# Order of the work inside a step of the projection: bank copies and weight splits before the head norms

## What is computed

```
h = rms_norm(x, g_mix)
proj = h @ w_in            # q, k, v of 3 groups of 8 heads | 512 SSM channels | gate_a | gate_b
q = head_rms_norm(q) * 64**-0.5      # t * rsqrt(mean(t*t) + eps), 64 columns of a head at a time
k = head_rms_norm(k)
sigmoid(gate_a), sigmoid(gate_b)
```

## Time and profile before

| | |
|---|---|
| time, median of 3 runs | 4731.93 us (4725.41, 4731.93, 4736.51) |
| span of the profiled execution | 4720.7 us |
| the profiled execution's own time | not listed beside the runs; the median lies 11.2 us above its span |
| busy: TensorE matmul, weight load, VectorE, ScalarE, GpSimd | 4550.3, 3984.6, 3161.5, 2181.6, 923.1 us |
| granted TensorE clock, mean | 0.985 |
| the projection | 0 to about 1204 us |

### The profile page before, as it was taken

How to read it: one execution, slowest core, us unless ns; L and a number is a source line. 1 busy time by engine, 2 the same in 40 slices (tenths; PEclk the granted TensorE clock), 3 DMA queues, 4 the chain that set the end, 5 groups by cost and what they waited for, 6 DMA issues and landing times.

```text
span 4720.7 us, 76711 instructions
## 1 busy us (share of the span) xinstructions
PE 4550.3 (96%) x25756; PEld 3984.6 (84%) x25756; DVE 3161.5 (67%) x6216; ACT 2181.6 (46%) x3608; POOL 923.1 (20%) x911
## 2 busy tenths in 40 slices
PE   8999999999899989996999999999999999999998
PEld 6777787777789978785999999999988888999997
DVE  6668676674656678455555565666667777778887
ACT  4454444343256752232333343444445555556665
POOL 2332101444112001122011111111112111111111
PEclk9999999999999999998999999999999999999999
DMA  6887766555644445443455456565657657777777
GB/s 214 283 310 266 229 200 204 165 188 176 209 165 147 140 162 187 163 146 124 164 187 190 167 187 204 172 213 192 210 200 238 215 206 245 246 249 268 271 270 255
DMA packets 339406, 971.18 MB, mean 206 GB/s; under 512 B 42089, under 2 KB 75668, under 8 KB 301909
## 3 DMA queue, kind: packets, MB, share of 16 engines
q1 hardware_dynamic: 273784, 804.16, 48.3%
q0 software_dynamic: 28304, 88.03, 8.0%
q10 hardware_dynamic: 37085, 76.04, 4.5%
HBM read 772.82 MB, written 200.58 MB: 206 GB/s over the span
## 4 chain that ended last, share of the span: by engine, by line
PE 51%; DVE 1%; ACT 0%; issue 0%; DVEq 0%; POOL 0%; DMA 0%; ACTq 0%; SPq 0%; POOLq 0%
PE ex_d L2834 14%; PE ex_g L2801 11%; PE ex_g L2803 9%; PE ex_g L2797 7%; PE ex_d L2797 4%; PE ex_d L2828 3%; PE ex_d L2803 2%; PE ex_g L2778 1%; PE ex_d L2778 0%; DVE ex_x L2996 0%; PE ex_d L2809 0%; DVEq L2605 0%; ACT ex_wgh L2881 0%; ACT ex_x L2894 0%; DVE ex_y L3070 0%
## 5 line engine op out<-in xcount | busy, mean ns | idle before, releaser
L2803 PE MATMUL ex_g<-ex_x,ex_wgl 128*128 128x256 f32 (+12 forms) x3456 | 981.7, 284 | 0.0
L2801 PE MATMUL ex_g<-ex_x,ex_wgh 128*128 128x288 f32 (+5 forms) x3584 | 757.1, 303 | 2.4 <-DVE ex_x L2996 2.4
L2803 PEld LDWEIGHTS ex_g<-ex_x,ex_wgl 128*128 128x128 f32 x3456 | 653.6, 189 | 3.9
L2881 ACT ACTIVATE ex_wgh<-ex_wg 128x2048 fp32r<-128x2048 f32 x274 | 523.9, 1912 | 283.0 <-PE ex_g L2803 275.6
L2978 DVE TENSOR_TENSOR ex_wgl<-ex_wg,ex_wgh 128x2048 fp32r<-128x2048 f32 x274 | 626.7, 2287 | 41.3 <-ACT ex_wgh L2881 41.3
L2801 PEld LDWEIGHTS ex_g<-ex_x,ex_wgh 128*128 128x128 f32 x3584 | 593.8, 188 | 11.6 <-DVE ex_x L2996 2.8
L2797 PE MATMUL ex_g<-ex_x,ex_wgh 128*128 128x512 f32 (+6 forms) x1664 | 529.6, 377 | 1.0 <-DVE ex_t L3008 1.0
L699 PE MATMUL prj_p<-prj_wh,prj_ah 128*128 128x512 f32 x1136 | 453.1, 399 | 28.4 <-DVE prj_wl L902 22.8
L2746 POOL DMA_INDIRECT out<-ex_y,ex_cur x82 | 155.4, 1896 | 1509.4 <-ACT ex_y L2902 1241.7
L699 PE MATMUL prj_p<-prj_wh,prj_al 128*128 128x512 f32 x1136 | 446.1, 393 | 0.0
L699 PE MATMUL prj_p<-prj_wl,prj_ah 128*128 128x512 f32 x1136 | 445.9, 393 | 0.0
(11 more groups left out here) (453 smaller groups left out, 9483.2 us busy)
## 6 DMA issues: line engine op xcount, KB each, us to landing
ex_wg<-in_w_gu SPq DMA_DIRECT2D x276, 1024.0 KB, 5.1
ex_wd<-in_w_down SPq DMA_DIRECT2D x276, 512.0 KB, 6.2
qkv_d<-prj_o ACTq DMA_DIRECT2D x144, 256.0 KB, 2.6
sp_rows<-sums_d SPq DMA_DIRECT2D x125, 256.0 KB, 3.1
wo_spare<-qkv_d SPq DMA_DIRECT2D x40, 768.0 KB, 4.2
sp_rows<-in_w_in SPq DMA_DIRECT2D x113, 256.0 KB, 3.1
sp_early<-in_w_in SPq DMA_DIRECT2D x56, 512.0 KB, 5.5
sums_d<-sp_early SPq DMA_DIRECT2D x28, 1024.0 KB, 5.3
```

What stands on the lines that cost most here:

```text
L2801: pe.matmul(out[:, 0:size], h[:, k, j, :], x[:, k, 0:size], start=(k == 0 and x is xh), stop=False)
L2803: last = pe.matmul(out[:, 0:size], l[:, k, j, :], xh[:, k, 0:size], start=False, stop=(k == KD - 1))
L2881: act.activation(flat(wgh[f % 2][:, :, :, :]), flat(wg[f % RAW][:, :, :, :]), ACT.Copy).then_inc(wgh_ready, 1)
```

## The change

In the loop over g, ScalarE calls `leave` and `split` first, and roots, gates and squares behind them. VectorE calls `leave` and `split` first, and scales and means behind them. Nothing else is changed: the same instructions with the same semaphores, in another order.

```diff
 # ScalarE
                         high(2 * b)
                         high(2 * b + 1)
-                    head_roots(g - 3)
                     if g:
                         leave(g - 1)
-                    gate_out(g - 2)
-                    head_squares(g - 2)
                     if g < NSTEP:
                         for s in splits_at(g):
                             split(s)
+                    head_roots(g - 3)
+                    gate_out(g - 2)
+                    head_squares(g - 2)
                     while left and store_at(left[0]) <= g:
                         store(left.pop(0))
 # VectorE
                         low(2 * b)
                         low(2 * b + 1)
-                    head_scales(g - 3)
-                    head_means(g - 2)
                     if g:
                         leave(g - 1)
                     if g < NSTEP:
                         for s in splits_at(g):
                             split(s)
+                    head_scales(g - 3)
+                    head_means(g - 2)
                     if g in block_at:
                         low(block_at[g])
```

## The result

| | median of the runs, us | lowest to highest | ratio to before, 95% interval |
|---|---|---|---|
| before, beside it | 4730.77 (7 runs) | 4725.41 to 4736.51 | |
| after | 4744.22 (7 runs) | 4742.54 to 4745.84 | 1.0032 [1.0023, 1.0041] |
| before, beside the second comparison | 4726.90 (25 runs) | 4719.13 to 4733.51 | |
| after, second comparison (experiment `after_again`) | 4739.55 (11 runs) | 4730.80 to 4744.67 | 1.0028 [1.0019, 1.0037] |

A forecast was written before the change was run, and what follows sets the result against it. TensorE's matmuls, covering 96% of the span, bound the kernel; only 24.7 us of its waits were reachable. Terms 1.25 + 1.5 + 1.5 - 0.9 + 0 gave +3.3 us, on the median 4735.2 us; range 4720 to 4748.

The forecast's parts named there:

- The place on the queue: ScalarE, product 4: tile 16's store stands behind a root waiting for VectorE's mean, issued about 429.5 us, not 427.66.
- The ring: Four output tiles: VectorE's leave waits for an older store, blocking when landings take over 2.5 us, before only over 5.
- The landing: Time from a store's issue until its tile is free: 4.8 us for tile 16, so the leave starts at 434.3.
- The waits of the bursts: TensorE's added waits in five spells, 390 to 1045 us: +1.25, +1.5, +1.5, -0.9 and 0, together +3.3 us.
- Waits before 390 us: Weight loads waiting for `prj_wl` ahead of the head norms: 20.7 us, to stay unchanged within 2 us.
- Burst 1: Pair at 416 to 456 us: tile 22's splits come 1.25 us later, so TensorE waits 7.0 us, not 5.8.
- The count of 15 ring waits: VectorE's leave waiting for a store, 390 to 1045 us: 15 or more places, 10 us or more, against four with 3.9.
- the sum: Added TensorE waits over five spells, +3.3 us, put on the median to give 4735.2 us, +0.07%.
- A: Rival: landings don't matter, nothing blocks beyond what cancels; 4731 to 4732 us, chance 0.17.
- B: Rival: product 4's chain costs less and stores land fast, 5 x 1.9 = 9.5 us gained; 4722 us, chance 0.15.
- head start: VectorE's splits have one scale and mean fewer ahead, 1.9 us per spell of waits, at most 9.5 us of 24.7.
- C: Rival: landings stay near 4.8 us through products 5 and 6 in three spells, +13 us more; 4748 us, chance 0.15.

The follow-up runs named there:

- after_again: The changed kernel run once more, unchanged, in one job with a second profile of the kernel before: 4739.55 us, ratio 1.0028.
- hybrid: Against the kernel before, the new order only in iterations where VectorE does the leave: 4711.01 us with five output tiles, 4737.35 us with four.

## Why the prediction was right or wrong

**The place on the queue: right.** The store of tile 16 was put at 429.5 us, 1.9 behind the leave of tile 19; it went out 1.82 us behind it. The root no longer waits ahead of that leave. The roots' waits for means did not go away for all that: they moved behind the splits and grew in sum, from 107.3 to 128.3 us (390 to 1045 us). The ring was named as what eats the gain; it does (20.7 us of waits for 5.6), and a fifth tile takes most of the loss away.

**The landing: too short.** I took 4.8 us, the landing that ended the old wait, from a spell of 3.7 to 6.6. It was 6.8, and the leave of tile 20 came 8.78 us behind that of tile 19 where 6.7 was worked out. For tile 22 I took 3.7 us, the shortest of the earlier trace rows, without a reason; it did no harm, since that store went out 8 us behind the one before it, landed in 2.0 us and held up nothing. The other traffic of the spell is in SP's timeline of after:

```profile
431.71 0.38 SPq L508 DMA_DIRECT2D sums_d<-sp_early  x1
433.21 1.64 SPq L456 DMA_DIRECT2D prj_raw<-in_w_in  x2
434.91 0.62 SPq L593 DMA_DIRECT2D slots_d<-in_empty_slots  x1
437.16 0.96 SPq L502 DMA_DIRECT2D sp_early<-in_w_in  x2
```

These were issued around the store of 435.63; which of them lengthened it, if any, was not tried. The rule of the Trainium skill, "SBUF — State Buffer", "The DMA setup-cost knee", was rightly set aside: it gives 2.6 us for 256 KB, and its formula has no term for other traffic, so "whatever else runs" is the prediction's reading of it. In this burst a store took 6.8 us; the landings of 857 to 885 us, median 2.0, lie under it.

**The waits of the bursts: sum close, parts not.** Added waits on `prj_wl`, each kernel's first profile:

| burst (before's time) | predicted | measured | how |
|---|---|---|---|
| 440 | +1.25 | +1.4 | 2.74 + 4.17 + 0.32 against 5.8 |
| 520 | +1.5 | +2.7 | 3.30 + 1.16 + 2.89 against 4.6 |
| 770 | +1.5 | +0.8 | 6.3 against 5.5 |
| 856 | -0.9 | -0.5 | 2.31 + 0.49 against 2.84 + 0.49 |
| 1026 | 0 | +0.6 | 2.34 + 0.65 + 1.89 against 1.80 + 0.65 + 1.84 |

Together +5.0 against +3.3, and 29.6 us in all, inside the 24 to 31 named. Burst 1 agrees partly by luck: in place of three ring waits there was one of 5.08 us, whose landing was 2 us longer than taken. The count of 15 ring waits was too high (9 and 10), their sum of 10 us or more was right. Waits before 390 us were to stay within 2 us and grew by 2.6 in one profile; in the second pair they fell, 20.8 after and 21.6 before.

**The step that failed: the sum priced idle time at its own length.** It ended with "+3.3 us" of waits and had no term for TensorE's clock. The waits became longer, not more: 17 and 18 of them against 17, the longest 4.2 and 4.1 us where the earlier trace rows has 2.8 (3.8 in the second profile). The clock term, extra busy time for the same matmuls over the stretch, measured 8.5 and 5.4 us, more than the idle term (5.4 and 3.4). With it the stretch alone gives +9 to +14 us, and the medians +12.7 and +13.5. The sign was right, the size a quarter of what came, and so the chance of slower by over 0.2% should have been more than 0.17.

**The rivals.** A (landings don't matter, 4731 to 4732) fell: VectorE waited 20.7 us for them, and with a fifth tile both orders gain. B (full head start, 4722) is false for this kernel, though after on five tiles happens to run 4722.24, and the head start it was about is real: 4.1 us of waits between hybrid and before, both on five tiles, where 9.5 was the bound. C (4748, waits past 36 us) came near the time, but not by its mechanism: the waits stayed under 31 us.

**What stays open.** Why the order after is 5 us behind the order before on five tiles; the hybrid shows that it lies in the iterations in which ScalarE does the leave, not which wait of them. Why the landings grow from 2 to over 7 us. And what besides the length of a wait decides whether the clock falls behind it: the hybrid on four tiles lost 8 to 11 us of busy time in the stretch with no wait for `prj_wl` over 3.3 us.

## What to carry to other kernels

Where two in-order queues hand a tile back and forth, reorder both or neither, and follow the chain once around, from one use of a buffer over its store to its next use: if that is longer than the iterations that the ring covers, work put ahead only moves the wait. Buy the buffer first and the order afterwards: here the order alone cost 0.3%; the fifth tile alone gave 0.25%, and together with the reorder, kept to the iterations in which it helps, 0.37%. And give the sum of TensorE's waits a second term for its clock: compare the busy time over the same matmuls in two profiles of each kernel, and look behind the long waits first.

## What the hardware did that was not expected

- **A long wait costs more than itself.** Three waits of 4.8 to 6.2 us brought 7.0 us of slower matmuls with them, nine of 1.8 to 4.0 us only 3.5. Behind one wait of 4.17 us the granted clock of a 10 us window was 0.58. A wait of 2.3 us had the lower clock behind it in two runs and not in a third.
- **Issuing a store earlier did not always make it land earlier.** Stores of the same 256 KB took between 2.0 and 7.9 us from 390 to 1045 us in the runs here; issued ahead of the root it landed, in the spell around 785 us, later by as much as it was early.
- **One profile of this kernel is good only to some 5 us.** The point where the head norms begin was reached at 344.7 to 352.3 us by kernels that do the same work up to there.
